# Rotary key of a latent-attention layer: two products per k tile from packed low and high columns, and its rotation on VectorE moved behind the second head

## What is computed

```python
k_rope = p[..., KV_END:KR_END][:, :, None, :]
if ang is not None:
    k_rope = rope2d(k_rope, ang)
...
out = jnp.stack([x1 * cos - x2 * sin, x1 * sin + x2 * cos], axis=-2)
```

## Time and profile before

| | |
|---|---|
| median of the runs | 827.59 us |
| the profiled execution | 827.32 us, span of its instructions 825.3 us, mean granted clock 0.994 |
| TensorE (PE) busy | 805.4 us, 98% |
| VectorE (DVE) busy | 511.8 us, 62% |
| ScalarE (ACT) busy | 371.9 us, 45% |
| GpSimd (POOL) busy | 368.6 us, 45% |
| key on latents | 71.98 to 77.45 us |
| context products | 77.45 to 85.93 us |
| heads' queries and first convolution pieces | 85.93 to 117.3 us |

### The profile page before, as it was taken

One profiled execution on the slowest core, in us unless ns is written; L12 is line 12 of the kernel. 1 busy time (PEld: TensorE's weight loads), 2 busy tenths in 40 slices (PEclk: granted clock), 3 DMA queues, 4 the chain that ended last, 5 costly groups with the idle time before them and its releaser, 6 DMA issues.

```text
span 825.3 us, 11436 instructions
## 1 busy us (share of the span) xinstructions
PE 805.4 (98%) x3937; PEld 671.3 (81%) x3937; DVE 511.8 (62%) x649; ACT 371.9 (45%) x592; POOL 368.6 (45%) x193
## 2 busy tenths in 40 slices
PE   4999999999999999999999999999999999999997
PEld 3778888888888888888788988888888888888885
DVE  5877589688888388777205575455555556535535
ACT  7656575566666323223225654443344433221223
POOL 5325593535543445554534064444444442544430
PEclk9899999999999999999999999999999999999999
DMA  9742251111110887786263043332333321332212
GB/s 309 252 141 61 69 125 30 50 30 48 36 42 28 262 275 253 224 241 198 98 234 90 13 126 104 102 101 85 93 102 102 101 86 68 102 124 91 93 51 102
DMA packets 120289, 97.82 MB, mean 119 GB/s; under 512 B 13660, under 2 KB 106105, under 8 KB 120249
## 3 DMA queue, kind: packets, MB, share of 16 engines
q1 hardware_dynamic: 120137, 97.26, 38.5%
q10 hardware_dynamic: 112, 0.04, 0.0%
HBM read 95.17 MB, written 2.10 MB: 118 GB/s over the span
## 4 chain that ended last, share of the span: by engine, by line
PE 95%; DVE 2%; ACT 2%; DMA 1%; issue 0%; SPq 0%; DVEq 0%; ACTq 0%
PE ps L428 26%; PE ps L430 26%; PE ps L429 26%; PE ps L1762 8%; PE ps L1871 3%; PE ps L1860 2%; PE ps L1617 1%; DMA xt<-x_dram 1%; ACT work L749 1%; PE ps L1964 0%; PE ps L1908 0%; PE ps L1657 0%; PE ps L1916 0%; ACT parts L791 0%; DVE vs L1280 0%
## 5 line engine op out<-in xcount | busy, mean ns | idle before, releaser
L345 POOL TENSOR_TENSOR wlo<-raw,whi 128x1024 fp32r<-128x1024 f32 (+4 forms) x125 | 280.0, 2249 | 354.6 <-ACT whi L337 354.5
L428 PE MATMUL ps<-hhi,whi 128*128 128x512 f32 (+1 forms) x520 | 196.0, 377 | 0.2 <-DVE hlo L1476 0.2
L430 PE MATMUL ps<-hhi,wlo 128*128 128x512 f32 (+1 forms) x520 | 195.7, 376 | 0.0
L429 PE MATMUL ps<-hlo,whi 128*128 128x512 f32 (+1 forms) x520 | 195.5, 376 | 0.0
L337 ACT ACTIVATE whi<-raw 128x1024 fp32r<-128x1024 f32 (+4 forms) x125 | 118.3, 957 | 138.9 <-PE ps L430 48.8
L428 PEld LDWEIGHTS ps<-hhi,whi 128*128 128x128 f32 x520 | 97.8, 188 | 18.3 <-DVE hlo L1476 0.4
L430 PEld LDWEIGHTS ps<-hhi,wlo 128*128 128x128 f32 x520 | 97.8, 188 | 18.0
L429 PEld LDWEIGHTS ps<-hlo,whi 128*128 128x128 f32 x520 | 97.9, 188 | 17.7
L1502 DVE TENSOR_TENSOR raw<-raw,gbc 128x1024 f32<-128x1024 f32 x22 | 50.4, 2295 | 43.9 <-DMA raw<-w_down_dram 43.9
L1510 DVE SCALAR_TENSOR_TENSOR work<-ps,prm,work 128x511 f32<-128x511 f32 x44 | 33.0, 749 | 71.2 <-ACT work L1051 70.3
L1406 DVE SCALAR_TENSOR_TENSOR adacc<-ada,cvec,adacc 128x1024 f32<-128x1024 f32 x28 | 63.8, 2318 | 14.9 <-DMA ada<-w_ada_dram 14.9
(11 more groups left out here) (288 smaller groups left out, 1509.5 us busy)
## 6 DMA issues: line engine op xcount, KB each, us to landing
raw<-w_up_dram SPq DMA_DIRECT2D x88, 256.0 KB, 3.1
ada<-w_ada_dram SPq DMA_DIRECT2D x32, 512.0 KB, 6.1
raw<-w_in_dram SPq DMA_DIRECT2D x56, 256.0 KB, 4.4
raw<-w_down_dram SPq DMA_DIRECT2D x44, 256.0 KB, 2.8
adaraw<-w_ada_dram SPq DMA_DIRECT2D x32, 256.0 KB, 5.4
raw<-w_o_dram SPq DMA_DIRECT2D x16, 256.0 KB, 3.1
xt<-x_dram SPq DMA_DIRECT2D x4, 512.0 KB, 7.5
raw<-w_attn_out_dram SPq DMA_DIRECT2D x8, 256.0 KB, 2.9
```

Of the source, the lines that this page charges most:

```text
L345: ins = (engine or nc.gpsimd).tensor_tensor(out=l, in0=r, in1=h.bitcast(F32), op=ALU.subtract)
L428: pe.matmul(o, l[0], r[0], start=start, stop=False)
L429: pe.matmul(o, l[0], r[1], start=False, stop=False)
L430: return pe.matmul(o, l[1], r[0], start=False, stop=stop)
```

## The change

The weight of a key's k tile is stored otherwise, and used in two matmuls instead of three. `whi` holds zeros in columns 0 to 63 and the high parts (key, swapped key) in 64 to 127. `wlo` holds the low parts in columns 0 to 63 and a copy of the high parts in 64 to 127. The product of `wlo` with the token's high part gives lo by hi in partitions 0 to 63 and hi by hi in 64 to 127; that of `whi` with the token's low part adds hi by lo in 64 to 127 (`key_pair`). The two halves are added afterwards: ScalarE copies partitions 0 to 63 out of PSUM to `krot2` (latents, 64 x 512) and `kr_ctx` (context, 64 x 256), behind the split of U_CX0 and ahead of the squares, and VectorE adds them.

For the split of a unit ScalarE (`key_hi`) now does three instructions of 128, 64 and 64 columns in place of 384, 64 and 64, waits for them and copies 256 columns to `wlo`; GpSimd (`key_lo`) sets 256 columns to zero and does three differences of 128, 64 and 64 columns.

On VectorE the context's key (one add of 32 x 256) stays in front of the heads, behind the sum of `sqk`. The latents' key is a block of four operations, `rotary_key`, behind head 1's reciprocals: add the halves (64 x 512), multiply by sines (32 x 512), multiply by cosines, add. Waits on `kr` and `kr_hi` are renumbered; head 2 on TensorE waits for the context's add alone.

```diff
         def views(u, slot):
-            if isinstance(u, int) and U_KR <= u < U_KR + 2:
-                return headed_raw(slot, DT // 2), headed(whi, slot, DT // 2), headed(wlo, slot, DT // 2)
             if isinstance(u, int) and u in U_UQ:
                 return headed_raw(slot, 2 * QT), headed(whi, slot, 2 * QT), headed(wlo, slot, 2 * QT)
             if isinstance(u, int) and u < U_KR:
...
                 return plain(raw, slot % RAW), plain(ohi, slot), plain(olo, slot)
             return plain(raw, slot % RAW), plain(whi, slot), plain(wlo, slot)
+        def key_tiles(t, slot):
+            return t[:, slot, 0:DT // 2 * P].rearrange("p (k n) -> p k n", n=P)
+        def key_parts(v, at):
+            r = v[:, :, at + ROPE:at + 2 * ROPE].rearrange("p g (a h j) -> p g a h j", a=2, h=2)
+            return [v[:, :, at:at + ROPE], r[:, :, :, 0, :], r[:, :, :, 1, :]]
+        def key_hi(act, u, slot):
+            arrived(act, u, slot)
+            wait(act, w_used, u - SLOTS + 1)
+            for r, h in zip(headed_raw(slot, DT // 2), key_parts(key_tiles(whi, slot), NOPE)):
+                if h.shape[-1] == ROPE:
+                    r = r[:, :, NOPE:QK]
+                ins = nc.scalar.activation(h, r, ACT.Copy)
+            ins.then_inc(w_hi, 1)
+            act.wait_ge(w_hi, u + 1)
+            nc.scalar.activation(key_tiles(wlo, slot)[:, :, NOPE:P], key_tiles(whi, slot)[:, :, NOPE:P], ACT.Copy).then_inc(s("kr_hi"), 1)
+        def key_lo(pool, u, slot):
+            wait(pool, w_used, u - SLOTS + 1)
+            nc.gpsimd.memset(key_tiles(whi, slot)[:, :, 0:NOPE].bitcast(F32), 0.0).then_inc(s("chl_zero"), 1)
+            pool.wait_ge(w_hi, u + 1)
+            pool.wait_ge(s("chl_zero"), u - U_KR + 2)
+            for r, h, l in zip(headed_raw(slot, DT // 2), key_parts(key_tiles(whi, slot), NOPE), key_parts(key_tiles(wlo, slot), 0)):
+                if h.shape[-1] == ROPE:
+                    r = r[:, :, NOPE:QK]
+                ins = nc.gpsimd.tensor_tensor(out=l, in0=r, in1=h.bitcast(F32), op=ALU.subtract)
+            ins.then_inc(w_lo, 1)
         def split_hi(act, u, slot, free=None, gated=None):
             if gated is None:
...
             return small[:, g % 4:g % 4 + 1]
         conv_y = tab[:]
+        kr_ctx = cx0[:, 0:C]
         def conv_x(j):
...
             for k in range(2, DT):
                 latent_lo(k)
             pool.wait_ge(w_lo, U_KR)
-            for u in range(U_KR, U_UQ[2]):
+            for u in range(U_KR, U_KR + 2):
+                key_lo(pool, u, u % SLOTS)
+            for u in range(U_KR + 2, U_UQ[2]):
                 split_lo(pool, u, u % SLOTS)
             for h in range(HEADS):
...
                 if c_ < 3:
                     token_rms(TT + c_ - 1)
             for u in (U_KR, U_KR + 1):
-                split_hi(act, u, u % SLOTS)
+                key_hi(act, u, u % SLOTS)
             def first_keys_raw(part):
                 lo, hi = ((0, T), (T, K))[part]
...
             for u in (*U_UQ[0:2], U_CX0):
                 split_hi(act, u, u % SLOTS)
+            used(act, U_KR + 1)
+            nc.scalar.activation(krot2[NOPE:P, :], ps[0:NOPE, 3, :], ACT.Copy).then_inc(s("kr_hi"), 1)
+            nc.scalar.activation(kr_ctx[NOPE:P, :], ps[0:NOPE, 0, 0:C], ACT.Copy).then_inc(s("kr_hi"), 1)
             for m in range(KVT):
                 act.wait_ge(s("lat_ps"), QT + KVT + m + 1)
                 nc.scalar.activation(sqk[m], wide(4 + 2 * m), ACT.Square).then_inc(s("p_sq"), 1)
...
             def rotary_key_hi(b):
-                act.wait_ge(s("kr"), 4)
+                act.wait_ge(s("kr"), 5)
                 nc.scalar.activation(khi[NOPE:QK, b, :], krot[NOPE:QK, :], ACT.Copy).then_inc(s("kr_hi"), 1)
             def conv_x_copy(j):
...
                     wait(dve, s("q_sum"), m - 1)
                     nc.vector.tensor_tensor(out=work[:, 3, :], in0=work[:, 3, :], in1=work[:, 3 + m, :], op=ALU.add).then_inc(s("q_sum"), 1)
-            dve.wait_ge(s("kr_ps"), 1)
-            dve.wait_ge(s("tab_loaded"), 16)
-            kr, tmp = krot[NOPE:QK, :], krot2[NOPE:QK, :]
-            kr_ps, kr_ctx = ps[:, 3, :], ps[:, 0, 0:C]
-            nc.vector.tensor_tensor(out=kr_ps[NOPE:QK, :], in0=kr_ps[NOPE:QK, :], in1=tab[NOPE:QK, :], op=ALU.mult).then_inc(s("kr"), 1)
             dve.wait_ge(s("p_sq"), QT + 2)
             nc.vector.tensor_tensor(out=sqk[0], in0=sqk[0], in1=sqk[1], op=ALU.add).then_inc(s("k_ssq"), 1)
+            kr, low = krot[NOPE:QK, :], krot2[NOPE:P, :]
+            dve.wait_ge(s("q_sum"), QT - 1)
             used(dve, U_KR + 1)
-            nc.vector.tensor_tensor(out=tmp, in0=kr_ps[QK:P, :], in1=tab[QK:P, :], op=ALU.mult).then_inc(s("kr"), 1)
-            nc.vector.tensor_copy(kr[:, T:K], kr_ctx[NOPE:QK, :]).then_inc(s("kr"), 1)
-            dve.wait_ge(s("kr"), 3)
-            nc.vector.tensor_tensor(out=kr[:, 0:T], in0=kr_ps[NOPE:QK, :], in1=tmp, op=ALU.add).then_inc(s("kr"), 1)
+            dve.wait_ge(s("kr_hi"), 4)
+            nc.vector.tensor_tensor(out=kr[:, T:K], in0=ps[NOPE:QK, 0, 0:C], in1=kr_ctx[NOPE:QK, :], op=ALU.add).then_inc(s("kr"), 1)
+            def rotary_key():
+                dve.wait_ge(s("tab_loaded"), 16)
+                nc.vector.tensor_tensor(out=ps[NOPE:P, 3, :], in0=ps[NOPE:P, 3, :], in1=low, op=ALU.add).then_inc(s("kr"), 1)
+                dve.wait_ge(s("kr"), 2)
+                nc.vector.tensor_tensor(out=krot2[QK:P, :], in0=ps[QK:P, 3, :], in1=tab[QK:P, :], op=ALU.mult).then_inc(s("kr"), 1)
+                nc.vector.tensor_tensor(out=ps[NOPE:QK, 3, :], in0=ps[NOPE:QK, 3, :], in1=tab[NOPE:QK, :], op=ALU.mult).then_inc(s("kr"), 1)
+                dve.wait_ge(s("kr"), 4)
+                nc.vector.tensor_tensor(out=kr[:, 0:T], in0=ps[NOPE:QK, 3, :], in1=krot2[QK:P, :], op=ALU.add).then_inc(s("kr"), 1)
             def rotary_key_lo(b):
-                dve.wait_ge(s("kr_hi"), b + 1)
+                dve.wait_ge(s("kr_hi"), b + 5)
                 nc.vector.tensor_tensor(out=klo[NOPE:QK, b, :], in0=kr, in1=khi[NOPE:QK, b, :].bitcast(F32),
                                         op=ALU.subtract).then_inc(s("kr"), 1)
...
                     nc.vector.reciprocal(q_scale, q_rms).then_inc(s("q_rinv"), 1)
                     dve.wait_ge(s("k_rms"), 1)
                     nc.vector.reciprocal(k_inv, k_rms).then_inc(s("k_rinv"), 1)
+                    rotary_key()
                 if 3 <= h < 3 + KVT:
                     m = h - 3
...
                     token_columns(TT + c_ - 1)
+            def key_pair(o, slot, k, hi, lo):
+                at = slice(k % 4 * P, (k % 4 + 1) * P)
+                pe.matmul(o, wlo[:, slot, at], hi[:, k, :], start=k == 0, stop=False)
+                return pe.matmul(o, whi[:, slot, at], lo[:, k, :], start=False, stop=k == DT - 1)
             pe.wait_ge(s("mods1"), 2 * DT)
             for n in range(2):
                 u = U_KR + n
                 unit(u)
-                last = project(pe, ps[:, 3, :], u % SLOTS, hhi[:, 4 * n:4 * n + 4, :], hlo[:, 4 * n:4 * n + 4, :], kt=DT // 2,
-                               start=n == 0, stop=n == 1)
-            last.then_inc(s("kr_ps"), 1)
+                pe.wait_ge(s("kr_hi"), n + 1)
+                for k in range(4 * n, 4 * n + 4):
+                    key_pair(ps[:, 3, :], u % SLOTS, k, hhi, hlo)
             pe.wait_ge(s("xT_low"), KT)
             pe.wait_ge(s("xT_up"), KT)
...
                                (chi[:, k, :], clo[:, k, :]), k == 0, k == DT - 1)
                     if k == DT - 1:
                         last.then_inc(s("lat_ps"), 1)
-                last = mm3(pe, ps[:, 0, 0:C], (tile_of(whi, u % SLOTS, k % 4), tile_of(wlo, u % SLOTS, k % 4)),
-                           (chi[:, k, :], clo[:, k, :]), k == 0, k == DT - 1)
+                last = key_pair(ps[:, 0, 0:C], u % SLOTS, k, chi, clo)
                 if k % 4 == 3:
                     last.then_inc(w_used, 1)
...
             for h in range(HEADS):
                 unit(U_UQ[h // 2])
                 if h == 2:
-                    pe.wait_ge(s("kr"), 3)
+                    pe.wait_ge(s("kr"), 1)
                 wait(pe, s("q_rope"), 3 * (h - 2))
                 wait(pe, s("q_nope"), h - 2)
                 slot = U_UQ[h // 2] % SLOTS
...
             pe.wait_ge(s("ck_lo"), KVT)
             pe.wait_ge(s("ck_t"), KVT)
-            pe.wait_ge(s("kr"), 4)
+            pe.wait_ge(s("kr"), 5)
             def values(kt):
...
                 if g == 0:
                     pe.wait_ge(s("q_lo"), HEADS)
                     pe.wait_ge(s("k_raw"), 2)
-                    pe.wait_ge(s("kr"), 5)
+                    pe.wait_ge(s("kr"), 6)
                     pe.wait_ge(s("v_lo"), KT - 2)
                 if g == 1:
                     pe.wait_ge(s("v_lo"), KT - 1)
                 if g == TT:
-                    pe.wait_ge(s("kr"), 6)
+                    pe.wait_ge(s("kr"), 7)
                 pe.wait_ge(s(("k_lo_even", "k_lo_odd")[h % 2]), h // 2 + 1)
```

## The result

| | before | after |
|---|---|---|
| median of five runs | 827.59 us | 832.18 us |
| lowest and highest | 827.25 to 828.3 | 831.36 to 832.96 |
| profiled execution, its span | 827.32, 825.3 | 832.18, 830.1 |
| TensorE busy, instructions | 805.4 us, 3937 | 808.6 us, 3921 |

The ratio is 1.0054, 95% interval 1.0043 to 1.0066: slower by 4.6 us. The forecast was 828.0 in 826.9 to 829.1.

A forecast was written before the change was run, and what follows sets the result against it. TensorE, busy 98% of the span, was taken as the bound. Its 2.77 us saving is lost in waits for the first cqlo and last ckraw copy, netting +0.45: 827.59 + 0.45 = 828.0 us, range 826.9 to 829.1.

The forecast's parts named there:

- the second pause: Second head: TensorE waits 2.2 us ahead of the query sums for ScalarE's last ckraw copy, taking all the saving.
- the clock falls in the new pauses: Rival: the pause ahead of the query sums lowers TensorE's granted clock, costing 1.9 us, total 829.9; chance 0.05.
- the pause of 0.77 did nothing: Argument against a clock fall: the longest earlier pause behind the start, at 54.92, left the granted clock at 0.9 and more.
- the two stalls: TensorE waits for the first cqlo near 75.6 and ahead of the query sums, 3.2 us together in 14.
- TensorE's saving: Key products on latents (1.82) and context (0.94), 16 instead of 24 each: 2.77 us if TensorE never waits.
- ScalarE's unit: Splitting the second key unit on ScalarE takes longer by 0.16 to 0.26 us, taken as +0.2.
- VectorE's block: Four rotary operations behind head 1's reciprocals, 2.9 us from near 94.9, hidden in idle time before heads 2 and 3.
- Pause two's release: TensorE goes on at the second head's query sums at about 89.82, after the last ckraw copy ends at 89.78.
- The two copies: ScalarE's added copies out of PSUM, ahead of the squares, delay them by 0.76 us (0.6 to 0.9).
- Pause one: At the context products TensorE waits 1.0 us (0.8 to 1.3) for VectorE's first cqlo, ready at 76.6.
- it waits 2.2 us: TensorE would reach the second head's query sums at 87.6 and wait until about 89.82.
- the prediction's +0.45: Net delay at the second head's query sums, 89.82 - 89.37, carried to the kernel's end.

The follow-up runs named there:

- experiment 1: Changed kernel with useless TensorE products filling both pauses, only that near 76 us, or only that ahead of the query sums: 828.94, 832.51, 828.71 us.
- fill_first: Changed kernel with only the pause near 76 us filled, by five useless TensorE products: 832.51 us, ratio to before 1.0059.
- fill_second: Changed kernel with only the pause ahead of the query sums filled, head 1's first six products made twice: 828.71 us, ratio to before 1.0009.
- best: copies_late plus context key products behind the key-value rank's 48 on TensorE and first query unit split earlier on ScalarE: 824.69 us, ratio to before 0.9965.
- fill_both: Changed kernel with both pauses filled, by five useless products and by head 1's first six products made twice: 828.94 us, ratio to before 1.0017.
- before_order: Kernel before, three key products kept, with context key products behind the others and the first query unit split early: 827.87 us, ratio 1.0003.
- best_front: best with the rotary_key block on VectorE in front of the heads instead of behind head 1: 825.67 us, ratio to before 0.9979.
- scalar_alone: Kernel before with only ScalarE's two added copies out of PSUM, ahead of the squares, into rows nobody reads: 828.48 us, ratio 1.0009.
- copies_late: Changed kernel with ScalarE's two copies of the key's low rows moved behind the ckraw copies: 827.84 us, ratio to before 1.0011.
- before_two: Kernel before with the key's third product left out, nothing packed, key less exact: 827.15 us, ratio 0.9993.
- best_late_unit: best without the early split of the first query unit on ScalarE: 828.18 us, ratio to before 1.0009.
- two_delay: before_two with ScalarE's first square made once more, delaying the last ckraw copy: 831.72 us, ratio to before 1.0042.
- before_delay: Kernel before with ScalarE's first square made three times more, delaying the last ckraw copy: 831.27 us, ratio 1.0047.

## Why the prediction was wrong

**The step that failed.** The sum charges the second pause with its length and puts what it does to the clock at nothing; that was left to the rival "the clock falls in the new pauses", chance 0.05. The clock falls: in the profiled run by the windows, in the other four by their times (831.36 to 832.96) and their mean granted clock (0.988 to 0.991, where before has 0.992 to 0.998). The argument against it was "the pause of 0.77 did nothing, and between the two stalls TensorE is busy without a gap". A pause of 0.77 says nothing of one of 1.4, and experiment 1 shows that the first pause isn't needed: fill_first has one pause and falls, fill_second has the first one of 1.09 and one of 0.26 and doesn't. The rival's price was mis-sized too: 1.9 us from nine products at the start, 3.2 measured, since the low level lasted 6.8 us here and the prediction took the 4.0 that were left of one in start-up. From the profiled execution of before, 827.32 + 0.6 + 3.2 + 1.1 = 832.2, the profiled one of after; the prediction had a term for the first 0.6 only.

**Right.** TensorE's saving, 2.77: best shows 2.74. ScalarE's unit: +0.2 expected, +0.24. VectorE's block: 2.9 expected, 99.08 + 0.69 - 96.87 = 2.90, and hidden; it began at 96.87 and not at 94.9, with the slow stretch in front of it, and head 3 still had 3.08 idle.

**Right by luck.** Pause two's release: 89.82 expected, 89.89 measured, but out of errors that cancelled. The conv weight's DMA was issued 0.56 later than before (80.69 against 80.13, 0.2 expected), behind ScalarE's query units, 0.57 later. Its split began 4.16 behind the issue, where it was 4.84 before, so at 84.85, 0.12 earlier than before. The two copies, 0.76 (0.6 to 0.9) expected, pushed the squares back by 1.97 - 0.96 = 1.01: the first starts behind the end of the split (85.94, end 85.91) and the square behind the end of the second (86.82, end 86.80), so overlaps that the sum had counted on are missing.

**Mis-sized.** Pause one: `cqlo` starts at 76.22, 0.57 later than before where +0.2 was expected. 0.33 of that is the second key unit's split, released by its DMA at 68.38 instead of 68.05, and 0.24 the unit. TensorE then starts not at the first `cqlo`'s end, as the sum has it, but 0.26 behind it (76.22 + 0.74 = 76.96, estimated from the 0.74 of a single one). So the context products came at 77.22 where 76.6 was expected. From the last key product's turn (72.21 + 16 x 0.229 = 75.87) that is 1.35 against 1.0 (0.8 to 1.3); the 1.20 in brackets counts from the last product's end. The context part ends at 84.87, not 84.15, so TensorE's turn at the sums comes at 88.3 (last product at 88.07) and not at 87.6, and "it waits 2.2 us" became 1.6, or 1.42 in brackets. None of this moved the release.

The Trainium skill (TensorE: Matmul & The Clock Gate, HAM oscillation), weighed in the prediction as a possibility without a term, says that work which pauses long enough goes back to half rate. The traces agree with that, and show that 1.4 us can be long enough. The page's limit for a harmless gap would let every pause of these kernels pass; the measurement decides against it.

**How often.** "Lifted" are the runs that stand apart from a kernel's lower group, by some 1.5 us or more, or, for after and fill_first, all of them (over fill_both and fill_second by 3). Only profiled runs show the stretch itself, and the pauses are theirs; the others are told by their time. The mean granted clock of each run bears it out: 27 of the 33 lifted runs have 0.990 or less, and none of the 164 others that the table counts has less than 0.991.

| kernel | pause 1, pause 2 (us) | lifted |
|---|---|---|
| before, all runs beside these kernels | none | 0 of 83 |
| before_order, best, best_front | none in head 1 | 0 of 25 |
| fill_second | 1.09, 0.26 | 0 of 10 |
| scalar_alone | none, 0.39 | 0 of 10 |
| fill_both | none, 0.52 | 1 of 10 |
| copies_late | 1.09, 0.56 | 4 of 10 |
| before_two | 0.87, 0.74 | 1 of 10 |
| best_late_unit | none, 1.22 | 5 of 10 |
| two_delay | 0.83, 1.38 | 8 of 10 |
| after | 1.20, 1.42 | 5 of 5 |
| fill_first | none, 2.00 | 4 of 4 |
| before_delay | none, 2.02 | 5 of 10 |

The share rises with the length of the second pause, but not by length alone: before_delay has the longest and falls in half of its runs, and a first pause may add to it (copies_late has 4 of 10, fill_both 1 of 10, with second pauses as long), which ten runs each can't settle. What decides in one run and not in the next stays open. The Trainium skill (TensorE: Matmul & The Clock Gate, What's actually happening) says that the moment at which the clock rises in warm-up depends on a phase that the kernel doesn't set. If the fall has that phase too, one pause could matter in one run and not in the next; no run here tests it.

A second thing stays open: kernels with short pauses and no fall are slower than the terms say. fill_both is +1.1 over before against the prediction's +0.45, scalar_alone +1.0 where 0.3 to 0.4 was expected. In fill_both's profiled run (827.66, its fastest) the sums come at 89.83, +0.46; no row shows the rest.

## What to carry to other kernels

Taking products from an engine that is busy 98% brings only what the waits just behind them allow; compute for each wait how far its feeder is ahead, and move the feeders' work first (here two copies moved back by 3 us, one split moved forward and TensorE's order were worth 7.5 us together). In a kernel that runs densely a new pause of one to two microseconds is not priced at its own length: add 3 us or more times a chance. Ahead of the sums of head 1 that chance was nothing up to 0.4 us, one to four runs in ten at 0.5 to 0.7 and half or more from 1.2 us on; a pause of 1.1 at the other place, with 0.26 ahead of the sums, had none in ten. That a shorter pause did nothing is no evidence against it.

## What the runs showed of the hardware

The clock can fall well behind the pause. In the four profiles with a fall, two_delay, after, fill_first and before_delay, the pause ended at 89.20, 89.89, 90.81 and 92.13, and the clock fell at 90.9, 92.1, 92.7 and 92.1. Three times that is 1.7 to 2.3 us later, in the middle of dense products, once it is at the pause's end. So a busy TensorE at 0.50 has to be followed back to an earlier gap.

The low level lasted 10.2, 6.8, 6.8 and 10.2 us, and the longer kind costs more. From the sums to the keys it is 28.0 us in before (89.37 to 117.37), 31.25 and 31.3 in after and fill_first, 32.8 and 32.9 in two_delay and before_delay: 3.3 us for the shorter kind and 4.9 for the longer.

At the start of the program the same level comes and goes at other times from run to run: it ends at about 26.3 in before, 27.3 in after and 28.2 in copies_late. Their key products start at 71.98, 72.21 and 72.79. This limits how well two profiles can be subtracted; that the clock at the start is what moves the key products is likely but not shown.
